# Two-layer streaming trunk on one core: finer hand-over of the first expert's weight slot, and a first gather by single row blocks

## What is computed

```python
g_prob = softmax(xt @ wg + bg);  g_top_p, g_idx = top_k(g_prob, 1)        # 1 of 4 groups
e_logits = (xt @ we + be)[chosen group];  e_top_l, e_idx = top_k(e_logits, 2)   # 2 of its 8 experts
gates = softmax(e_top_l) * g_top_p
out[token] = sum over its 2 experts of gate * ((silu(x @ w_gate[e]) * (x @ w_up[e])) @ w_down[e])
```

## Time and profile before

| | |
|---|---|
| median of 3 runs | 1272.65 us (1272.19 to 1274.26) |
| the profiled execution | 1272.65 us, its span 1270.9 us |
| PE busy / its weight loads busy | 1048.5 us (83%) / 712.1 us (56%) |
| DVE / ScalarE / GpSimd busy | 477.2 us (38%) / 234.7 us (18%) / 4.9 us |
| HBM read | 459.38 MB, mean 362 GB/s over the span |
| chain that ended last | PE 55%, DMA 40%, rest 5% |

### The profile page before, as it was taken

One profiled execution on the slowest core, in us unless ns is written; L12 is line 12 of the kernel. 1 busy time (PEld: TensorE's weight loads), 2 busy tenths in 40 slices (PEclk: granted clock), 3 DMA queues, 4 the chain that ended last, 5 costly groups with the idle time before them and its releaser, 6 DMA issues.

```text
span 1270.9 us, 22379 instructions
## 1 busy us (share of the span) xinstructions
PE 1048.5 (83%) x9528; PEld 712.1 (56%) x9528; DVE 477.2 (38%) x1227; ACT 234.7 (18%) x526; POOL 4.9 (0%) x27
## 2 busy tenths in 40 slices
PE   9999998966777575799999999998977676758685
PEld 7888755634433342448888888865544343424243
DVE  2342543342223222236665556464344222222232
ACT  2221121111111111113433334121111111111111
POOL 1000000000000000000000000000000000000000
PEclk9999998878788887899999999999898778878799
DMA  9888699999999999995666664999999999999996
GB/s 343 235 336 330 234 422 429 425 429 429 429 429 428 429 429 429 426 392 186 207 216 226 223 215 149 348 344 418 428 428 428 430 428 429 429 428 429 429 426 278
DMA packets 96049, 461.49 MB, mean 363 GB/s; under 512 B 17260, under 2 KB 60520, under 8 KB 70632
## 3 DMA queue, kind: packets, MB, share of 16 engines
q1 hardware_dynamic: 95616, 460.34, 90.1%
q10 hardware_dynamic: 360, 0.15, 0.0%
HBM read 459.38 MB, written 1.08 MB: 362 GB/s over the span
## 4 chain that ended last, share of the span: by engine, by line
PE 55%; DMA 40%; DVE 1%; issue 1%; SPq 1%; ACT 1%; POOL 0%; POOLq 0%; DVEq 0%; ACTq 0%
DMA front<-in_expert_w_up 33%; PE pa L1767 10%; PE pa L1487 10%; PE pb L1487 8%; DMA arena<-in_expert_w_down 5%; PE wa L1767 5%; PE acc L1518 4%; PE wb L1792 3%; PE acc L1625 2%; PE pb L1735 2%; PE acc L1802 1%; PE pb L1551 1%; PE pb L1726 1%; SPq L356 1%; PE pb L1836 1%
## 5 line engine op out<-in xcount | busy, mean ns | idle before, releaser
L1767 PE MATMUL pa<-front,arena 128*32 128x256 f32 x1792 | 137.0, 473 | 90.7 <-DMA front<-in_expert_w_up 90.7
L1767 PEld LDWEIGHTS pa<-front,arena 128*32 128x32 f32 x1792 | 66.7, 135 | 163.4 <-DMA front<-in_expert_w_up 103.2
L1245 DVE TENSOR_SCALAR lower<-lower 128x128 f32<-128x128 f32 x64 | 14.4, 225 | 382.6 <-ACT lower L583 382.6
L1767 PE MATMUL wa<-front,arena 128*32 128x256 f32 x1248 | 93.5, 463 | 64.5 <-DMA front<-in_expert_w_up 60.8
L1767 PEld LDWEIGHTS wa<-front,arena 128*32 128x32 f32 x1248 | 45.6, 132 | 112.8 <-DMA front<-in_expert_w_up 69.6
L583 ACT ACTIVATE arena<-wb 32x256 f32<-32x256 f32 (+2 forms) x236 | 88.9, 377 | 105.6 <-PE wb L1792 96.8
L1792 PE MATMUL wb<-w_dn,conv_raw 128*32 128x256 f32 x1472 | 87.8, 379 | 2.5 <-DMA w_dn<-in_expert_w_down 2.5
L1735 PE MATMUL pb<-arena,hs 128*128 128x128 f32 x448 | 67.6, 313 | 26.0 <-DVE arena L1161 11.3
L1487 PE MATMUL pa<-hnT,w_x 128*128 128x256 f32 x384 | 85.1, 380 | 0.0
L1735 PEld LDWEIGHTS pb<-arena,hs 128*128 128x128 f32 x448 | 61.7, 220 | 40.4 <-DVE arena L1177 18.6
L1487 PEld LDWEIGHTS pa<-hnT,w_x 128*128 128x128 f32 x384 | 72.5, 190 | 10.0 <-issue 0.3
(11 more groups left out here) (340 smaller groups left out, 1219.8 us busy)
## 6 DMA issues: line engine op xcount, KB each, us to landing
w_dn<-in_expert_w_down SPq DMA_DIRECT2D x46, 2048.0 KB, 26.0
front<-in_expert_w_gate SPq DMA_DIRECT2D x42, 2048.0 KB, 19.0
front<-in_expert_w_up SPq DMA_DIRECT2D x42, 2048.0 KB, 23.4
w_x<-in_expert_w_gate SPq DMA_DIRECT2D x15, 2048.0 KB, 30.3
w_x<-in_expert_w_up SPq DMA_DIRECT2D x15, 2048.0 KB, 34.6
arena<-in_expert_w_down SPq DMA_DIRECT2D x14, 2048.0 KB, 26.5
w_x<-in_odd_in_proj SPq DMA_DIRECT2D x16, 1024.0 KB, 5.4
front<-in_expert_w_up SPq DMA_DIRECT2D x8, 1024.0 KB, 9.3
```

The lines of the kernel that those rows point to most:

```text
L1245: link(v.tensor_scalar(eg, eg, 1.0, None, ALU.add))
L1767: ins = mm(gu[32 * j:32 * j + 32, :, :], xb[:, k, c0:c0 + CAP], w[k][:, :, P * j:P * j + P], start=(k == 0), stop=(k == KC - 1))
```

## The change

1. `early0` is laid out by row block (gate and up of one k together), so expert 0's first chunk can be given back in two halves. Its first page loads now write runs of 2 KB where they wrote 4 KB.
2. The quarter that goes there is loaded by two transfers of 512 KB, behind `gu_half` 1 and 2; `gu_half` now counts after k = 0, 1, 3 and 5 of expert 0 and in the middle of expert 1 (5 counts).
3. The first gather and its scaling go by single row blocks: 8 gathers, 8 `gathered_first` (a `tensor_scalar` of 128x128 in place of a `tensor_tensor` of 128x256), 8 runs of gate/up matmuls, and the 8 DVE calls are spread anew through the chain of small operations.
4. The first selection compares the ranks in PSUM, ahead of the multiplication by the mask. For that a token of the expert must be told from the others: 1000 (`FAR`) is added to the diagonal of `upper` and to `iota1` and `slot_id`, and taken off and put on again around layer 1's mixer (`raise_diagonal`, three DVE operations of 128x128).
5. `even_norm` computes the mean of each token tile ahead of the copy of its transposes; `warm(7)` becomes `warm(4)`.

```diff
-FIRST = 4
+FIRST = 5
+FAR = 1000
-        early0 = chunks(2, 3).rearrange("p (a g k f) -> p a g k f", a=3, g=2, k=2)
+        early0 = chunks(2, 3).rearrange("p (a k g f) -> p a k g f", a=3, g=2, k=2)
...
             def first_pages(l, e, part):
+                if e == 0:
+                    w = (expert_w_gate, expert_w_up)[part][l, e].rearrange("(p a k) f -> p a k f", a=4, k=2)
+                    sp_.dma_start(early0[:, :, part], w[:, 0:3]).then_inc(S["gu_in0"], 16)
+                    return
...
-                sp_.wait_ge(S["gu_half"], FIRST * l + 1)
-                quarter(l, 3, 0, 1, "gu_in0")
-                sp_.wait_ge(S["gu_half"], FIRST * l + 2)
+                for n in range(2):
+                    sp_.wait_ge(S["gu_half"], FIRST * l + n + 1)
+                    quarter(l, 3, 0, 1, "gu_in0", 2 * n, 2 * n + 2)
+                sp_.wait_ge(S["gu_half"], FIRST * l + 3)
                 quarter(l, 3, 1, 1, "gu_in0")
-                sp_.wait_ge(S["gu_half"], FIRST * l + 3)
+                sp_.wait_ge(S["gu_half"], FIRST * l + 4)
                 quarter(l, 4, 0, 0, "gu_in1")
-                sp_.wait_ge(S["gu_half"], FIRST * l + 4)
+                sp_.wait_ge(S["gu_half"], FIRST * l + 5)
...
+            def raise_diagonal(by):
+                link(v.scalar_tensor_tensor(upper[:, :], ident[:, :], float(by), upper[:, :], ALU.mult, ALU.add))
...
+                select_quad(0, prk)
                 v.tensor_tensor(pos, prk, mask, ALU.mult).then_inc(S["mask_done"], 1)
                 dve.wait_ge(S["mask_done"], 2 * l + 2)
-                select_quad(0)
...
                 link(v.scalar_tensor_tensor(s1, e2, 1.0, gs, ALU.add, ALU.mult))
+                gathered_first(l, 0)
                 link(v.reciprocal(g1, s1))
                 link(v.tensor_tensor(g2, g1, e2, ALU.mult))
-                gathered_first(l, 0)
+                gathered_first(l, 1)
...
                 link(ins)
+                gathered_first(l, 2)
                 link(v.tensor_tensor(gates, oh1, oh2, ALU.add))
-                gathered_first(l, 1)
...
                 link(v.tensor_scalar(prefer, descend[:, :], 1.0, None, ALU.add))
+                gathered_first(l, 3)
                 link(v.scalar_tensor_tensor(prefer, iota[:, :], float(PRE), prefer, ALU.is_ge, ALU.mult))
                 link(v.scalar_tensor_tensor(prefer, cnt, float(CAP), prefer, ALU.is_gt, ALU.mult))
-                gathered_first(l, 2)
                 link(v.tensor_tensor(prefer, prefer, wide, ALU.max))
                 link(v.tensor_reduce(out=most, in_=prefer, axis=AX, op=ALU.max))
+                gathered_first(l, 4)
...
                 link(v.tensor_scalar(keep, keep, -1.0, 1.0, ALU.mult, ALU.add))
-                gathered_first(l, 3)
+                gathered_first(l, 5)
                 link(v.tensor_tensor(cols2, cols, over(other), ALU.mult))
                 link(v.tensor_reduce(out=at_other[:, 0:6], in_=cols2, axis=AX, op=ALU.add))
                 link(v.tensor_tensor(cols2, over(other), along(cols[:, :, WIDE:WIDE + 1]), ALU.mult))
+                gathered_first(l, 6)
                 link(v.tensor_tensor(cols, cols, over(keep), ALU.mult))
                 link(v.tensor_tensor(cols, cols, cols2, ALU.add))
                 link(v.tensor_tensor(cols2, over(here), along(at_other[:, 0:6].unsqueeze(2)), ALU.mult))
+                gathered_first(l, 7)
                 link(v.tensor_tensor(cols, cols, cols2, ALU.add))
...
-            def gathered_first(l, part):
-                dve.wait_ge(S["gath_done"], PARTS * l + part + 1)
-                k = slice(2 * part, 2 * part + 2)
-                v.tensor_tensor(xs[:, k, :], (XG, XG1)[part % 2][:, 0:2, :],
-                                nffn[:, l, k].unsqueeze(2).to_broadcast([P, 2, QUAD * CAP]), ALU.mult
+            def gathered_first(l, k):
+                dve.wait_ge(S["gath_done"], PARTS * l + k + 1)
+                v.tensor_scalar(xs[:, k, :], (XG, XG1)[k % 2][:, 0, :], nffn[:, l, k:k + 1], None, ALU.mult
                                 ).then_inc(S["xs_done"], 1)
...
             def first_gate_up(l):
                 gather_first(l, 0)
                 gather_first(l, 1)
-                for part in range(FIRST):
-                    if 0 < part < FIRST - 1:
-                        gather_first(l, part + 1)
-                    pe.wait_ge(S["xs_done"], PARTS * l + part + 1)
-                    ins = gate_up(xs, 0, early_cols(0), GU[0], ks=(2 * part, 2 * part + 1))
-                    if part < FIRST - 1:
+                pe.wait_ge(S["mask_done"], 2 * l + 2)
+                for k in range(KC):
+                    if 0 < k < KC - 1:
+                        gather_first(l, k + 1)
+                    pe.wait_ge(S["xs_done"], PARTS * l + k + 1)
+                    ins = gate_up(xs, 0, early_cols(0), GU[0], ks=(k,))
+                    if k in (0, 1, 3, 5):
                         ins.then_inc(S["gu_half"], 1)
                 ins.then_inc(S["gu_done"], 1)
...
-                    warm(7)
+                    warm(4)
```

More of the change, by code:

```diff
@@ L911, in even_norm, with mean @@
                 v.tensor_copy(norm_w[:, :, :].rearrange("p a k -> p (a k)"), acc[:, 3, 256:288]).then_inc(S["norm_cols"], 1)
[L912 to L915, removed]
+                def mean(t):
                     dve.wait_ge(S["x_sq"], t + 1)
@@ L918, in even_norm, with turned_in @@
                                     ).then_inc(S["mean_sq"], 1)
+                def turned_in(i):
+                    dve.wait_ge(S["x_t"], i + 1)
+                    v.tensor_copy(resT[:, 4 * i:4 * i + 4, 0:P], (pa, pb)[i][:, :].rearrange("p (k m) -> p k m", k=4)
+                                  ).then_inc(S["x_raw_dve"], 1)
+                mean(0)
+                turned_in(0)
+                mean(1)
+                turned_in(1)
                 dve.wait_ge(S["norm_cols"], 1)
@@ L1276, in moe @@
                         gathered(q + 1, l, 1)
+                    if l == 0 and e == LISTED - 1:
+                        raise_diagonal(-FAR)
                     if e == LISTED:
@@ L1444, in _ @@
             odd_mix(ODD_UNITS - 1)
+            raise_diagonal(FAR)
             residual_mixer(1)
@@ L1731, in gather_quad @@
                     pe.wait_ge(S["g4_done"], NE * l + QUAD * q)
-                pe.wait_ge(S["xs_done"], PARTS * l + FIRST + 2 * (q - 1) + half)
+                pe.wait_ge(S["xs_done"], PARTS * l + KC + 2 * (q - 1) + half)
                 for k in range(KC // 2):
@@ L1748, in late_cols, with gather_first @@
                 return [(late3, late4)[e - 3][:, k // 4, :, k % 4, :] for k in range(KC)]
-            def gather_first(l, part):
-                if part == 0:
+            def gather_first(l, k):
+                if k == 0:
                     pe.wait_ge(S["quad_sel"], NE // QUAD * l + 1)
                     pe.wait_ge(S["hs_done"], 4 * l + 4)
-                if part > 1:
-                    pe.wait_ge(S["xs_done"], PARTS * l + part - 1)
-                for k in (2 * part, 2 * part + 1):
-                    for t in range(TT):
-                        ins = mm((XG, XG1)[part % 2][:, k % 2, :], hs[:, t, k, :], quad_slots[:, t, :],
-                                 start=(t == 0), stop=(t == TT - 1))
+                if k > 1:
+                    pe.wait_ge(S["xs_done"], PARTS * l + k - 1)
+                for t in range(TT):
+                    ins = mm((XG, XG1)[k % 2][:, 0, :], hs[:, t, k, :], quad_slots[:, t, :],
+                             start=(t == 0), stop=(t == TT - 1))
                 ins.then_inc(S["gath_done"], 1)
@@ L1876, in middle_quad @@
                     pe.wait_ge((S["gu_in0"], S["gu_in1"], S["gu_in2"])[s],
-                               32 * each * q + (32 * loads + (48 * (l + 1), 32 * (l + 1), 32)[s]))
+                               32 * each * q + (32 * loads + (48 * (l + 1) + 16 * (l + 1), 32 * (l + 1), 32)[s]))
                     gate_up(xs, CAP * j, gu_cols(s), GU[j % 2],
-                            2 * q + (PARTS * l + FIRST - 2) if j == 0 else None).then_inc(S["gu_done"], 1)
+                            2 * q + (PARTS * l + KC - 2) if j == 0 else None).then_inc(S["gu_done"], 1)
                     loads = uses(DSLOT, d, NE) * l + uses(DSLOT, d, before + 1) - LOOP[0]
```

27 lines of the change are left out of this document (15 added, 12 removed).

## The result

| | before | after |
|---|---|---|
| median, same chip | 1272.65 us (1271.05 to 1276.07, 11 runs) | 1279.02 us (from 1274.62, 11 runs) |
| ratio, 95% interval | | 1.0041 (1.0028 to 1.0054) |
| the profiled execution / its span | 1272.65 / 1270.9 us | 1276.89 / 1275.1 us |
| PE busy / DVE busy | 1048.5 / 477.2 us | 1051.1 / 479.7 us |

The change makes the kernel slower, by 5.2 us at the ratio; the forecast was 1273.6 us with a range to 1276.0. (Single executions of 5713.98 us here, and of 3542.71 and 1286.21 us in b_swap, stand far off the others and carry no argument.)

The account below looks back on a forecast made before the run. The prediction took the stream of expert loads, at its edge at expert 4's release, as the bound. Terms of +1.15, +0.55 and -0.7 us made +1.0 us on 1272.65, so 1273.6 us, range 1270.3 to 1276.0 us.

Parts of the forecast that it names:

- The bound: Expert stages: a stream of loads sets the end, and the release at expert 4 is already at its edge.
- The first release: Expert 0's first chunk: SP issues 1.4 us earlier, at 147.1 us; the stream before 184 us gains some 0.9 us.
- The end of the first expert: Expert 0: DVE's new order makes PE end at 155.3 us against 153.5 now, 1.8 us later.
- the first rival: Expert 0: PE's hand-overs, 8 more at 0.08 us, set its end, 0.4 us later; 1270.9 us; chance 0.14.
- The chain from there: Expert 0 to expert 4: nothing absorbs the lateness; expert 6's issue moves from 184.18 to 186.0 us.
- The start-up: Expert 6's load on an empty stream: lands 8.35 us after issue; +1.15 us in layer 0, +0.55 in layer 1.
- the dummies: Dummy matmuls, warm(7) to warm(4): three fewer of 0.24 us, less their overlap, -0.7 us.
- the even_norm order: Mean ahead of the copy: GpSimd starts earlier, but V's weights are next; gain 0 to 0.1 us, taken as 0.
- the operations on the diagonal: Three operations around the mixer, some 0.35 us each: hidden, costing 0.35 us each only if that cover were gone.
- the runs of 2 KB: First page loads in runs of 2 KB: hidden, as both are issued long before the experts.
- the late release: Rival at expert 4: scalings take 0.344 us of room and start-up is 9.25 us; 1276.5 us; chance 0.17.
- the early stream: Rival: the earlier stream carries through, each layer keeping up to 1.4 us; 1269.1 us; chance 0.14.

Follow-up runs that it names:

- b_swap: Kernel before, with only the second quad's first gather moved to the other bank, behind expert 3's SwiGLU product; 1271.64 us, ratio 0.9994.
- b_wait9: Kernel before, with 9 dummy matmuls behind expert 0's last gate/up matmuls in both layers; 1278.97 us, ratio 1.0041.
- b_wait18: Kernel before, with 18 dummy matmuls behind the first expert in each layer; 1281.85 us, ratio 1.0053.
- c_swap: Kernel before, with release by halves, comparison in PSUM, first scaling ahead of reciprocal, warm(4), and second quad's first gather in the other bank; 1269.83 us, 0.9970.
- a_dve: Changed kernel, with the last two scalings moved ahead of more of DVE's chain of small operations; 1274.45 us, 1.0006 times the kernel before.
- the second measurement: Changed kernel timed again without an edit, against the kernel before on one chip; 1276.76 us, ratio 1.0017.
- b_psum: Kernel before, with only the comparison in PSUM, the first scaling ahead of the reciprocal, and warm(4); 1273.16 us, ratio 0.9991.
- b_half: Kernel before, with only the layout by row block and the two 512 KB transfers; 1273.39 us, ratio 0.9994.

## Why the prediction was wrong

- **The bound**: right. The stream is on the edge at expert 4. Later costs about one to one in layer 0 and less in layer 1 (b_wait9, b_wait18), earlier gives next to nothing in layer 0 (b_swap, c_swap: issues 1.2 and 2.4 us earlier, landings at 193.5 and 193.3 us where it was 193.2).
- **The first release**: right within 0.1 us. The first 512 KB goes at 147.18 (forecast 147.1). Some of that is luck: the 0.30 us that the forecast puts between DVE's scaling and PE were PE's own work on the next gather, and measure 0.15. That the stream would gain 0.9 us up to 184 us was wrong. It was ahead by 0.96 us at 159.8 us and lost most of that at the middle of expert 1, whose release came 1.91 us late; the forecast had passed this one over. The load ahead of expert 6's landed 0.2 us later, not 0.9 earlier. The sum used the gain only to call the queue empty there.
- **The end of the first expert**: the number held (155.42 for 155.3, +1.91 for +1.8). DVE does release the last run of gate/up, at 154.78 (forecast 154.8), with its last scaling at 154.38 (forecast 154.15). But it is not what made expert 0 long: PE alone would have been ready only 0.59 us sooner, and a_dve is just 0.46 us shorter. The term that was mis-sized is PE's hand-over in the first rival, 0.08 us, taken from the gap between a gather's end and DVE's start. It is 0.17 us per group, so with no wait for DVE PE would be late by 1.32 - 0.24, about 1.1 us, not by 0.4.
- **The chain from there**: this is the step that failed. "So expert 6's issue moves from 184.18 to 186.0 us" supposes PE at full clock as in the one profile of before. Expert 1 started at 155.24 us, and 30.83 us later is 186.07; the actual issue was 187.36, for 3.4 us of low clock behind an idle PE. That term, 1.27 us in the profiled execution, stood at nothing. With it the sum takes 0.65 us off the lateness in layer 0, since a later load would land sooner after its issue (8.35 us for 9.0); its landing does, but by the layer's end 3.0 of the 3.2 us are back.
- **The start-up**: taken 8.35 us, measured 8.1 and 8.4. Landings +2.3 in layer 0 (forecast +1.15, the rest the clock) and +1.15 in layer 1 behind its own offset of 2.95 (forecast +0.55: 2.03 for 1.8, and the 0.34 us at SP). The figure of the Trainium skill ("DMA: Bandwidth & Descriptors", section "Anatomy of one DMA", an estimate of 6.8 us, fitted there on another issue path) is too short for this one, as the 8.5 us of the load at 99.72 us already said.
- **Sum on the profiled execution**: +2.3, +0.7 in layer 0's stream behind that (its last load lands 3.0 us late; not traced further), -0.5 for the dummies (forecast -0.7), +0.45 in layer 1's mixer (not traced), +1.15: 4.1 of the 4.2 us. The forecast had nothing for the 0.7 and the 0.45.
- **The median** is another 2 us above that execution, while the ratio of the second measurement would put it at 1272.65 x 1.0017 = 1274.8 us, inside the range. Executions of the changed kernel reach 1282 us. The range was built from one profile's terms and had no term for the clock, which added 1.3 or 2.7 us wherever it fell in the chain. How much of the median's 6.4 us is the clock is not known.
- **No effect seen**: the even_norm order (V's first matmul at 9.38 us in both), the operations on the diagonal (b_psum), the runs of 2 KB (b_half). The Trainium skill ("VectorE: DVE Perf Modes", section "The TRN2 errata") says that many small tiles pay a fixed price each on VectorE, for sources in SBUF. Here the source is PSUM, and the trace agrees in kind: a scaling of 128 columns takes 0.35 us where 256 took 0.42. But the larger price fell on PE's groups.
- **Rivals**: the late release was the right kind, but with other causes: it counted on longer scalings and a start-up of 9.25 us, and neither came. Against the early stream stand b_swap and c_swap in layer 0, whose earlier issues landed no earlier.

Open: whether the change makes low clock in the chain more likely, or whether it is met there by chance. It lay there in 8 of 22 stretches with the idle microsecond and in none of 6 without it. That fits an idle PE bringing it on, but is too few to show it, and those 6 are also 2.2 us shorter.

## What to carry to other kernels

When a stream of loads is fed on the edge, find the instructions whose ends release the next loads, each of them, and count what stands on their engine ahead of them. A finer hand-over that starts the stream earlier is worth nothing if it makes that chain longer. Going back and forth between two kinds of matmuls in smaller groups cost PE time per group here, so read the period of one part from start to start, not the length of its operations or the idle time. A release without slack also turns a drop of the clock into lost time: 2 us of idle PE removed there were worth 2.2 us by medians, more than any part of this change, and c_swap, which has it, is the one kernel that is clearly faster.

## What the runs showed of the hardware

- Alternating gathers and gate/up matmuls on PE costs 0.17 us per group over groups twice as long: gathers of 4 stand 0.64 us apart from what follows and of 8 1.09, gate/up groups of 8 0.57 and of 16 1.00. Gate/up behind gate/up, with a semaphore wait already met, has 0.88 for 16.
- The granted clock drops to 0.50 (1.2 GHz) for 3.4, 6.8 or 10.2 us at a time, again and again in every profile. 3.4 us of it made 16 matmuls of 128x128 take 3.36 in place of 2.02 us. Where it falls differs from execution to execution of the same kernel.
- A scaling of 128x128 from PSUM takes 0.35 us and 0.27 us of room; 512 KB on an idle queue landed after 4.1 us (after, 147.18) and 1 MB after 5.0; 2 MB issued at most 2.3 us before the load ahead of it landed took 7.8 to 8.6 us, and once 10.0 (b_wait18, layer 0).
